# First mixer: one product and the sum of the decay-free weights made by VectorE, the steps joined one slot later

## What is computed

```python
cum = jnp.cumsum(lac, axis=1)
decay = jnp.exp(jnp.where(causal, cum[:, :, None] - cum[:, None], -jnp.inf))
xdt = xc * dtc[..., None]
cb = jnp.einsum('blgn,bsgn->blsg', cc, bc)
y = jnp.einsum('blsgr,bsgrp->blgrp', cb[..., None] * decay, xdt)
y = y + jnp.einsum('blgn,bgrpn->blgrp', cc, state) * jnp.exp(cum)[..., None]
```

## Time and profile before

| | |
|---|---|
| median of three runs | 1842.42 us (1839.36 to 1845.85) |
| profiled execution | 1839.35 us, span 1837.6 us, mean granted clock 0.97 |
| TensorE | busy 1703.0 us (93%) |
| VectorE | 1107.7 us (60%) |
| ScalarE | 842.0 us (46%) |
| GpSimd | 362.3 us (20%) |
| GpSimd's products (line 726) | 64, 75.4 us |
| GpSimd's joins (line 710) | 32, 45.3 us; idle before them 232.4 us, for ScalarE (line 914) |
| VectorE's `mm` (line 1058) | 32, 31.2 us; idle before them 68.8 us, for GpSimd (line 730) |

### The profile page before, as it was taken

One profiled execution on the slowest core, in us unless ns is written; L12 is line 12 of the kernel. 1 busy time (PEld: TensorE's weight loads), 2 busy tenths in 40 slices (PEclk: granted clock), 3 DMA queues, 4 the chain that ended last, 5 costly groups with the idle time before them and its releaser, 6 DMA issues.

```text
span 1837.6 us, 20988 instructions
## 1 busy us (share of the span) xinstructions
PE 1703.0 (93%) x7944; PEld 1368.1 (74%) x7944; DVE 1107.7 (60%) x1520; ACT 842.0 (46%) x1365; POOL 362.3 (20%) x299
## 2 busy tenths in 40 slices
PE   6878898898887999999998899999999999999998
PEld 4766676686665768888776677888678778888886
DVE  6666666667576757574747666776655653434343
ACT  5655565465543453444445235446354442414232
POOL 0253434444354000000004401222120110000001
PEclk9989999999998999999999999999999999999999
DMA  3633443443321222222222223222323233333331
GB/s 103 177 118 96 116 130 103 126 114 103 93 72 48 81 58 80 70 72 78 69 59 85 68 65 74 63 68 80 102 81 104 83 89 102 93 98 98 93 102 69
DMA packets 260106, 164.58 MB, mean 90 GB/s; under 512 B 26909, under 2 KB 249286, under 8 KB 258982
## 3 DMA queue, kind: packets, MB, share of 16 engines
q1 hardware_dynamic: 260006, 163.25, 31.0%
HBM read 160.86 MB, written 2.36 MB: 89 GB/s over the span
## 4 chain that ended last, share of the span: by engine, by line
PE 65%; DVE 12%; issue 9%; ACT 6%; POOL 5%; DMA 2%; SPq 1%; ACTq 0%; POOLq 0%; DVEq 0%
PE stream L79 18%; PE stream L81 18%; PE stream L80 18%; ACT weights_hi L137 2%; DVE weights_lo L147 2%; POOL ssd_work L726 2%; PE q L775 1%; DVE ssd_x L980 1%; PE q L1962 1%; PE q L1986 1%; DMA ssd_exp_cum<-ssd_cum_pairs 1%; POOL ssd_work L730 1%; PE q L79 1%; PE q L81 1%; PE q L80 1%
## 5 line engine op out<-in xcount | busy, mean ns | idle before, releaser
L79 PE MATMUL stream<-u_lo,weights_hi 128*128 128x512 f32 (+2 forms) x1312 | 532.2, 406 | 11.5 <-DVE u_lo L249 4.5
L80 PE MATMUL stream<-u_hi,weights_lo 128*128 128x512 f32 (+2 forms) x1312 | 515.2, 393 | 0.0
L81 PE MATMUL stream<-u_hi,weights_hi 128*128 128x512 f32 (+2 forms) x1312 | 515.2, 393 | 0.0
L137 ACT ACTIVATE weights_hi<-weights_raw 128x1024 fp32r<-128x1024 f32 (+4 forms) x269 | 268.7, 1001 | 499.1 <-PE stream L81 473.1
L147 DVE TENSOR_TENSOR weights_lo<-weights_raw,weights_hi 128x1024 fp32r<-128x1024 f32 (+4 forms) x269 | 323.2, 1203 | 278.0 <-ACT weights_hi L137 277.7
L79 PEld LDWEIGHTS stream<-u_lo,weights_hi 128*128 128x128 f32 (+2 forms) x1312 | 248.2, 189 | 77.9 <-issue 9.3
L80 PEld LDWEIGHTS stream<-u_hi,weights_lo 128*128 128x128 f32 (+2 forms) x1312 | 247.9, 189 | 54.6 <-issue 4.9
L81 PEld LDWEIGHTS stream<-u_hi,weights_hi 128*128 128x128 f32 (+2 forms) x1312 | 247.4, 189 | 55.2 <-issue 0.7
L217 POOL COPY h_sum_of_squares<-h_squares 128x512 f32<-128x512 f32 x5 | 3.2, 649 | 795.3 <-ACT h_squares L205 795.3
L79 PE MATMUL stream<-ssd_y_lo,weights_hi 128*128 128x512 f32 x128 | 61.0, 477 | 45.2 <-DVE ssd_x L980 33.2
L79 PE MATMUL stream<-mlp_a_lo,weights_hi 128*128 128x512 f32 x256 | 100.2, 391 | 0.0
(11 more groups left out here) (460 smaller groups left out, 2925.6 us busy)
## 6 DMA issues: line engine op xcount, KB each, us to landing
weights_raw<-in_w_mlp_dram SPq DMA_DIRECT2D x64, 512.0 KB, 3.8
weights_raw<-in_ssd_w_in_dram SPq DMA_DIRECT2D x48, 512.0 KB, 4.1
weights_raw<-in_gla_w_in_dram SPq DMA_DIRECT2D x40, 512.0 KB, 3.8
ssd_cum_steps<-ssd_cum_rows SPq DMA_DIRECT2D x32, 512.0 KB, 4.9
weights_raw<-in_w_in_dram SPq DMA_DIRECT2D x29, 512.0 KB, 3.8
ssd_exp_cum<-ssd_cum_pairs SPq DMA_DIRECT2D x16, 512.0 KB, 7.6
weights_raw<-in_ssd_w_out_dram SPq DMA_DIRECT2D x16, 512.0 KB, 3.6
weights_raw<-in_gla_w_out_dram SPq DMA_DIRECT2D x13, 512.0 KB, 3.4
```

What stands on the lines that cost most here:

```text
L79: pe.matmul(out, lh, rl, start=first, stop=False, skip_group_check=skip)
L80: pe.matmul(out, ll, rh, start=False, stop=False, skip_group_check=skip)
L81: return pe.matmul(out, lh, rh, start=False, stop=last, skip_group_check=skip)
L137: act.activation(w_view(c, n)[0], raw_view(c, n), ACT.Copy).then_inc(c.w_rounded, 1)
```

## The change

GpSimd keeps one of the two products (the backward one, `t2`), one operation per step where it had three. It waits for VectorE's sum of the step before, which read `t2`. VectorE makes the other product (`t1`), adds `t2` to it and multiplies with the decay; `s_m` now counts these three operations, so all waits on it are scaled by 3. `work` holds two tiles instead of three. The joins get a table `JOIN` of their own, one slot behind `CUT`, and the decays move one slot with them; in GpSimd's program the joins now stand behind the slot's product, except in slot 7, where they stay ahead of `complete`. ScalarE takes the exponentials of line 880 in slots 4 and 5 instead of 2 and 5.

```diff
-        work = mb("work", [P, 3, T])
+        work = mb("work", [P, 2, T])
+        t1, t2 = work[:, 0, :], work[:, 1, :]
...
-        DECAY = {(1, 0): ((0, 0), (0, 1)), (1, 1): ((0, 2), (0, 3))}
+        JOIN = {(1, 0): ((0, 0), (0, 1)), (1, 1): ((0, 2), (0, 3))}
+        DECAY = {(1, 1): ((0, 0), (0, 1)), (1, 2): ((0, 2), (0, 3))}
         for g in range(1, SG):
-            for t, cut, decay in ((0, (g, 3), (g, 4)), (1, (g, 4), (g, 5)), (2, (g, 5), (g, 6)),
-                                   (3, (g, 6), (g + 1, 0))):
+            for t, cut, join, decay in ((0, (g, 3), (g, 4), (g, 5)), (1, (g, 4), (g, 5), (g, 6)),
+                                        (2, (g, 5), (g, 6), (g + 1, 0)), (3, (g, 6), (g, 7), (g + 1, 1))):
...
                 if j >= RING:
-                    sp.wait_ge(s_m, j - RING + 1)
+                    sp.wait_ge(s_m, 3 * (j - RING + 1))
...
+            def join_steps(i, k):
+                for pg, t in JOIN.get((i, k), ()):
+                    pool.wait_ge(s_cut, 4 * pg + t + 1)
+                    flat_steps = [steps[:, (4 * pg + t) % RING, d, :, :].rearrange("p h l -> p (h l)") for d in range(2)]
+                    pool.tensor_tensor(flat_steps[0], flat_steps[0], flat_steps[1], ALU.add).then_inc(s_join, 1)
...
                 if k == 7:
+                    join_steps(i, k)
                     complete(g, 0)
                 if 2 <= k <= 5:
 
                     t = k - 2
                     pool.wait_ge(s_cbm, 2 * g + 2)
...
-                    for d in range(2):
-                        if d and n:
-                            pool.wait_ge(s_t2, 3 * n)
-                        pool.tensor_tensor(ways[d].rearrange("p (h l) -> p h l", h=HPG),
-                                           again(cbm[:, d, t * P:(t + 1) * P], HPG),
-                                           spread(head(dtc, d, t, g), P), ALU.mult).then_inc(s_t2, 1)
-                    pool.wait_ge(s_t2, 3 * n + 2)
-                    pool.tensor_tensor(ways[0], ways[0], ways[1], ALU.add).then_inc(s_t2, 1)
...
+                    if g or t:
+                        pool.wait_ge(s_m, 3 * (4 * g + t) - 1)
+                    pool.tensor_tensor(t2.rearrange("p (h l) -> p h l", h=HPG),
+                                       again(cbm[:, 1, t * P:(t + 1) * P], HPG),
+                                       spread(head(dtc, 1, t, g), P), ALU.mult).then_inc(s_t2, 1)
+                if k < 7:
+                    join_steps(i, k)
...
-                if k in (2, 5) and g in G:
-                    p = (k - 2) // 3
+                if k in (4, 5) and g in G:
+                    p = k - 4
...
                     t = k - 2
-                    dve.wait_ge(s_t2, 3 * (4 * g + t + 1))
+                    m = 3 * (4 * g + t)
+                    v = t1.rearrange("p (h l) -> p h l", h=HPG)
+                    if t == 0:
+                        dve.wait_ge(s_cbm, 2 * g + 2)
+                    if 4 * g + t:
+                        dve.wait_ge(s_m, m)
+                    dve.tensor_tensor(v, again(cbm[:, 0, t * P:(t + 1) * P], HPG),
+                                      spread(head(dtc, 0, t, g), P), ALU.mult).then_inc(s_m, 1)
+                    dve.wait_ge(s_m, m + 1)
+                    dve.wait_ge(s_t2, 4 * g + t + 1)
+                    dve.tensor_tensor(t1, t1, t2, ALU.add).then_inc(s_m, 1)
+                    dve.wait_ge(s_m, m + 2)
                     dve.wait_ge(s_decay, 4 * g + t + 1)
...
-                    dve.tensor_tensor(mm[:, t % 2, :, :].rearrange("p h l -> p (h l)"), work[:, t % 2, :],
+                    dve.tensor_tensor(mm[:, t % 2, :, :].rearrange("p h l -> p (h l)"), t1,
```

More of the change, by code:

```diff
@@ L600, in ssd_stage @@
         CUT = {(0, 7): ((0, 0), (0, 1)), (1, 0): ((0, 2), (0, 3))}
-        DECAY = {(1, 0): ((0, 0), (0, 1)), (1, 1): ((0, 2), (0, 3))}
+        JOIN = {(1, 0): ((0, 0), (0, 1)), (1, 1): ((0, 2), (0, 3))}
+        DECAY = {(1, 1): ((0, 0), (0, 1)), (1, 2): ((0, 2), (0, 3))}
         for g in range(1, SG):
-            for t, cut, decay in ((0, (g, 3), (g, 4)), (1, (g, 4), (g, 5)), (2, (g, 5), (g, 6)),
-                                   (3, (g, 6), (g + 1, 0))):
-                CUT[cut] = CUT.get(cut, ()) + ((g, t),)
-                DECAY[decay] = DECAY.get(decay, ()) + ((g, t),)
+            for t, cut, join, decay in ((0, (g, 3), (g, 4), (g, 5)), (1, (g, 4), (g, 5), (g, 6)),
+                                        (2, (g, 5), (g, 6), (g + 1, 0)), (3, (g, 6), (g, 7), (g + 1, 1))):
+                for table, slot in ((CUT, cut), (JOIN, join), (DECAY, decay)):
+                    table[slot] = table.get(slot, ()) + ((g, t),)
         def conv_tile(g, j):
@@ L718, in _ @@
                     pool.wait_ge(s_cbm, 2 * g + 2)
[L719 to L722, removed]
-                    for d in range(2):
-                        if d and n:
-                            pool.wait_ge(s_t2, 3 * n)
-                        pool.tensor_tensor(ways[d].rearrange("p (h l) -> p h l", h=HPG),
-                                           again(cbm[:, d, t * P:(t + 1) * P], HPG),
-                                           spread(head(dtc, d, t, g), P), ALU.mult).then_inc(s_t2, 1)
-                    pool.wait_ge(s_t2, 3 * n + 2)
-                    pool.tensor_tensor(ways[0], ways[0], ways[1], ALU.add).then_inc(s_t2, 1)
-            c.second_mixer_set_up(pool, [(s_nrm, SG), (s_y, 4 * SG), (s_st, 7 * SG), (s_m, 4 * SG)])
+                    if g or t:
[4 more added lines that the diff above has]
+                if k < 7:
+                    join_steps(i, k)
+            c.second_mixer_set_up(pool, [(s_nrm, SG), (s_y, 4 * SG), (s_st, 7 * SG), (s_m, 12 * SG)])
             add_squares(c, pool)
@@ L736, in y_intra @@
             def y_intra(g, t):
-                pe.wait_ge(s_m, 4 * g + t + 1)
+                pe.wait_ge(s_m, 3 * (4 * g + t + 1))
                 if t == 0:
@@ L1022, in _ @@
                     if g:
-                        dve.wait_ge(s_t2, 12 * g)
+                        dve.wait_ge(s_t2, 4 * g)
                     else:
```

## The result

The changed kernel takes 1824.72 us, the median of four runs (1823.13 to 1826.80); the kernel before, run beside it, 1843.74 us (1839.36 to 1845.85).

A forecast was written before the change was run, and what follows sets the result against it. TensorE was taken to bound the kernel, stalled by VectorE's late taps behind GpSimd's join. Inner rounds 11 plus round 1's 2.5 less round 8's 1.1 made 12.4 us off 1842.42: 1830.0 us, range 1811 to 1841.

The forecast's parts named there:

- The stall for the taps: TensorE's wait at slot 4's third output tile in each inner round: from 5.42 to 1.2 us.
- slot 5 is next: New TensorE stall of 3.3 us ahead of slot 5 for the closing of tile 1; slot 5 starts 3.1 us earlier.
- the pair: VectorE's two small state products in slot 4 collide with GpSimd's product and join: some 2.7 us instead of 0.75.
- The inner rounds: Rounds 2 to 7: 1.8 us gained per round, 11 us over six (8.4 to 18.6).
- The clock in single rounds: A fall after slot 5's stall loses 1.7 us: per inner round 3.1 us gained without it, 1.4 with it.
- Round 1: Chain to its end comes 2.6 us earlier, stall before 120.70 stays and grows: gain 2.5 us.
- Round 8: VectorE sets the pace; slot 4 starts 1.4 us earlier, then five times 0.73 and collisions: loss 1.1 us.
- moving the exponentials: Line 880 from slot 2 to 4: costs nothing in inner rounds; in round 8, slot 4 starts 1.4 us earlier.
- (a): Collision at slot 4's state pair missed or small: 5.0 us gained per round, 1810 us; chance 0.19.
- (b): GpSimd's product goes first at handover from sum to `mm`, holding VectorE 1.0 us in slot 3: 1841 us; chance 0.14.
- (c): VectorE's product on two repeated operands takes twice a plain one, on top of (b): 1853 us; chance 0.08.
- (d): A join still waits ahead of a product; slot 4's third tile still starts about 290: 1842 us; chance 0.03.

The follow-up runs named there:

- two kernels with joins held: Changed kernel with slot 5's join held until slot 4's state sum, 1817.35 us; that plus two tiles for `t2` and joins of slots 4 and 6 held, 1803.18 us.
- the fastest version: Kernel before with joins behind products and a slot later, exponentials moved, GpSimd keeping both products and sum, joins of slots 4 to 6 held: 1783.36 us, ratio 0.9675.
- the two other versions without a fall in them: Kernel before with joins and decays later, exponentials moved: 1792.32 us; changed kernel with two tiles for `t2`, joins of slots 4 to 6 held: 1803.18 us.
- the split: Changed kernel with joins and decays back in their old places; VectorE's product and sum and the moved exponentials stay: 1821.53 us, ratio 0.9874.
- the order alone: Kernel before with joins behind products and a slot later, decays later, exponentials in slots 4 and 5; GpSimd keeps both products and sum: 1792.32 us, ratio 0.9717.
- the join of slot 5 held: Changed kernel with GpSimd's join of slot 5 waiting until VectorE's state sum of slot 4: 1817.35 us, ratio 0.9859.
- two buffers: Changed kernel with two tiles for `t2`, so GpSimd's product is made earlier, and joins of slots 4, 5 and 6 held: 1803.18 us, ratio 0.9779.

## Why the prediction was right, and where its steps were not

**Sign, place and mechanism** held. The stall for the taps is 1.19 us (walked: 1.2), because `mm` no longer waits for GpSimd; slot 5 is next, held by the closing of tile 1 (2.95 us, walked 3.3); the pair takes 2.68 us (walked: 2.7); VectorE is busy 48.9 us and GpSimd 18.1 us in a round (47 to 50, near 18). The 2.7 was added up from single operations; the kernel before had such a pair whole, in round 8, at 2.69 us. That the collision is on the path was argued then; two kernels with joins held showed it since.

**The inner rounds** gained 14.5 us, where I had 11. These two rows, of before and after, split it: TensorE's idling (the stretch less its busy time) fell from 33.8 to 25.3 us, its busy time, which is longer at the lower clock, from 355.3 to 349.3:

```profile
131.85:520.92 389.07, 355.30 (x1707) 280.18 (x1706) 254.06 (x361) 215.50 (x392) 165.62 (x133) 0.95 0.38 111
```

```profile
130.67:505.20 374.53, 349.26 (x1705) 276.64 (x1704) 293.58 (x409) 214.11 (x391) 108.54 (x84) 0.97 0.39 116
```

My sum in the same two parts was 5.5 us of idling (5.42 less 1.2 and 3.3 in each of six rounds) and the other 5.5 of clock. So the clock's part, 6.0 us, was near in total, and the idling's, 8.5 us, was 3.0 us too small: the new stall is 0.35 us shorter in each round than walked, since TensorE's own work up to slot 5 took 4.8 us and not 4.4; the stalls of the other rounds before were up to 0.2 us longer than that of the pattern, round 4; and round 3 had one more, of 0.5 us.

**The clock in single rounds** was mis-sized, though. Rounds 3 and 6, in which it didn't fall, gained 4.4 and 3.8 us, not 3.1; the four others, where it fell, 2.3, 0.8, 2.3 and 0.9 us, where I had 1.4 for all. In these rounds the fall has two sizes. Mean clock after the stall ahead of slot 5, in rounds 2, 4 and 3 (columns as in the earlier trace rows):

```profile
162.00:164.00 2.00, 2.00 (x5) 1.60 (x6) 2.00 (x3) 0.36 (x1) 1.20 (x1) 0.50 0.04 8
164.00:166.00 2.00, 2.00 (x8) 1.60 (x7) 1.93 (x4) 0.00 (x0) 0.00 (x0) 0.81 0.15 36
...
285.00:287.00 2.00, 1.73 (x4) 1.49 (x5) 2.00 (x4) 0.82 (x3) 1.28 (x1) 0.50 0.00 0
287.00:289.00 2.00, 2.00 (x6) 1.54 (x6) 1.97 (x3) 0.00 (x0) 0.00 (x0) 0.50 0.05 14
289.00:291.00 2.00, 2.00 (x7) 1.54 (x6) 1.93 (x5) 0.00 (x0) 0.00 (x0) 0.50 0.99 279
291.00:293.00 2.00, 2.00 (x10) 1.66 (x9) 0.18 (x1) 0.00 (x0) 0.00 (x0) 0.98 0.61 232
...
224.00:226.00 2.00, 1.79 (x8) 1.51 (x9) 2.00 (x4) 0.77 (x2) 1.30 (x1) 1.00 0.00 0
```

Added up over these rounds, the clock was at 1.2 GHz for some 3.4 us in rounds 2 and 5, for some 6.8 us in rounds 4 and 7, and for some 6.8 us, partly under the stall, in each of the six rounds of the kernel before. I had taken 1.7 us for every fall from a single place of round 1. Half of 3.4 and of 6.8 us is 1.7 and 3.4 us, and that orders the gains: about 4.1 us without a fall, 2.3 with the short one, 0.8 with the long one. The four falls together are 20.5 us, and half of that is 10.2. TensorE's busy time in these rounds is 10.2 us above that of the fastest version (349.3 against 339.1 us), but only 7.6 above that of the two other versions without a fall in them (341.7 and 341.6), so the size fits and is not exact. What decides between no fall, a short and a long one behind the same stall stays open.

**Round 1** was forecast to gain 2.5 us and gained 0.55. The chain I followed did come 2.55 us earlier, at 118.15 instead of 120.70. But 0.6 us of that lie ahead of the round's mark. And TensorE reached it earlier still, so its stall grew from 3.63 to 7.41 us; the granted clock fell under the stall already and was low until about 123.9 instead of 124.2, behind the stall for 5.7 us instead of 3.5, which takes back 1.1 us:

```profile
118.15 1.65 PE L776 MATMUL q<-ssd_bc,ssd_state 128*128 128x128 f32 x6 [7.41 <-DVE ssd_state_parts L966]
```

```profile
118.00:120.00 2.00, 1.85 (x7) 1.78 (x8) 0.56 (x2) 1.99 (x3) 1.68 (x2) 0.50 0.00 0
120.00:122.00 2.00, 2.00 (x6) 1.59 (x5) 0.00 (x0) 1.98 (x3) 0.86 (x2) 0.50 0.00 0
122.00:124.00 2.00, 2.00 (x6) 1.53 (x6) 0.28 (x1) 1.99 (x3) 0.73 (x1) 0.55 0.00 0
```

I had written that the stall stays and grows, but had not priced what follows it. Of the miss of 1.95 us some 0.2 us are untraced.

**Round 8** lost 0.4 us and not 1.1. The terms that I wrote down don't add up to 1.1: five times 0.73 less 1.4 is 2.3, before any collision. And I had counted on several collisions there; no group follows, so no join is left, and the state pair at 524.84 takes 1.60 us with only GpSimd's product in the way. In the kernel before, that pair took 2.69 us and the `mm` of slot 3 took 1.52 instead of 0.69. The last `mm` comes 0.3 us earlier behind the round's mark than before, not 1.1 later, and the loss arises behind it.

**The step that was wrong** is that moving the exponentials costs and gains nothing in the inner rounds. Both its runs speak against it: moved alone they are worth 0.6%, and without them the change is worth 0.2%. I judged ScalarE by its busy share (35.89 of 64.61 us), as I had warned against for VectorE, and not by who stands behind the waiting operation in its program. The walk came out all the same, because it left `yl` at its old place in the round, and it is the move that kept it there. In that the prediction had luck: the part that it priced at nothing carries most of the gain.

**The rivals.** (a) Collision small: false, the pair took 2.68 us. What it would have been worth is now measured, 21.5 us with both collisions gone. (b) GpSimd first at the handover from sum to `mm`: false. VectorE's `mm` is 0.69 us in slot 3, and GpSimd's product, released by the same sum, starts 0.11 us behind it and takes 1.48 us instead of 1.04. (c) A slow product on VectorE: false, 0.69 us. (d) false: GpSimd's idle time ahead of its joins no longer stands before a product.

**What the parts are worth.** Order and split are two cures for one wait, and they don't add. With the exponentials moved, which alone gives 0.6%, the order gives 2.8%, the split 1.3%, both together 1.0%. The split shortens GpSimd's work behind its late join; the order takes the join out of the way. Once one has been done, the other has nothing left to remove, and the split leaves its price: two operations of 0.7 us per slot on VectorE, whose closings TensorE then waits for, and a GpSimd product that is released right ahead of the state pair. Over the six rounds the changed kernel has 27 us more than the order alone, of which 19.5 us are TensorE's idling (25.3 against 5.8) and the rest the clock that falls after it.

The row that speaks on this choice is GpSimd's sum, 1.29 us against VectorE's 0.69. The Trainium skill, "GPSIMD Engine Reference", section 4.1 "Engine selection", has VectorE for an elementwise sum or product and calls GpSimd some two times slower. The times agree with it; the choice doesn't follow from them, since GpSimd had 37 us of a round to spare and VectorE's operations were on the path.

## What to carry to other kernels

Before work is moved from one engine to another, look at what stands ahead of it in its own engine's program: an operation that waits for something far away belongs behind the work that is ready, and that reordering gave 2.8% here where the move gave 1.3%, each with the exponentials moved. Place GpSimd's operations on SBUF under VectorE operations that read PSUM, not next to dependent ones that read two SBUF tiles; one added wait on an engine off the path, which held a join back, gained 0.4%. And when a stall goes, price the next one with its clock, not only with its length.

## What was unexpected about the hardware

- **The two engines alternate.** The pair of 128x256 state products took 0.75 us with GpSimd idle, 1.60 us with one GpSimd operation waiting, 2.68 us with two: each GpSimd operation ran once between two of VectorE's. Where a sum released both the next VectorE operation and a GpSimd product, VectorE's went first by 0.11 us, in all 24 such handovers of the changed kernel, and ran undisturbed at 0.69 us. The Trainium skill, "SBUF — State Buffer", section "Who interferes with whom", states that a VectorE instruction with two SBUF inputs contends with GpSimd instructions that read SBUF; the runs agree. The taps, which have one operand in PSUM, kept 3.10 us for four with and without a join beside them.
- **The fall of the clock doesn't follow from the stall's length alone.** After: 2.95 us ahead of slot 5 in each of six rounds, a fall in four of them. With the join of slot 5 held: 1.87 us there, and a fall in all six, of some 3.4 us each. With two buffers: 1.01 us there, behind 1.19 at the third tile, and none. Round 4 with the join held:

```profile
281.60:283.60 2.00, 1.93 (x6) 1.57 (x7) 2.00 (x3) 1.71 (x6) 1.43 (x2) 0.64 0.00 0
283.60:285.60 2.00, 2.00 (x6) 1.54 (x5) 1.97 (x3) 0.00 (x0) 1.39 (x1) 0.50 0.24 31
285.60:287.60 2.00, 2.00 (x10) 1.62 (x9) 1.97 (x4) 0.00 (x0) 0.00 (x0) 1.00 1.07 341
```

- **A product with both operands repeated costs no more than a plain one** of the same size: 0.69 us on VectorE, and on GpSimd less than a plain sum, 1.04 against 1.29 us, or than a plain product (line 701), 1.30 us.
